# Two transformer blocks on one core: the order of weight roundings, form copies and loads in a Strassen-type feed-forward stage

## The reference

```python
D_FF = (D_MODEL * 11) // 4            # 5632
def conv_ffn(h, up, conv_w, conv_b, down):
    hid = causal_dwconv(h @ up.astype(h.dtype), conv_w, conv_b)   # 3 taps along positions
    gate, val = jnp.split(hid, 2, axis=-1)
    return (jax.nn.gelu(gate) * val) @ down.astype(h.dtype)
...
        h = rms_norm(x, pre_ffn_norm[l])
        y = conv_ffn(h, ffn_up[l], ffn_conv_w[l], ffn_conv_b[l], ffn_down[l])
        x = x + rms_norm(y, post_ffn_norm[l])
```

## Time and profile before

| | |
|---|---|
| runs of the kernel | 2668.67 us median of 3 (2666.76 to 2669.28) |
| profiled execution, own time | 2666.55 us |
| its span, first to last instruction | 2664.6 us |
| mean granted clock of TensorE | 0.995 |
| TensorE busy | 2628.2 us (99%) |
| VectorE, ScalarE, GpSimd busy | 1827.3, 1137.3, 309.5 us |
| first up quad, about | 1361 to 1403 us of the span |
| down quads, about | 2180 to 2582 us |
| last segment, about | 2583 to 2665 us |

### The profile page before, as it was taken

One profiled execution on the slowest core, in us unless ns is written; L12 is line 12 of the kernel. 1 busy time (PEld: TensorE's weight loads), 2 busy tenths in 40 slices (PEclk: granted clock), 3 DMA queues, 4 the chain that ended last, 5 costly groups with the idle time before them and its releaser, 6 DMA issues. The chain is left out here.

```text
span 2664.6 us, 39524 instructions
## 1 busy us (share of the span) xinstructions
PE 2628.2 (99%) x17064; PEld 2291.9 (86%) x17064; DVE 1827.3 (69%) x1836; ACT 1137.3 (43%) x1183; POOL 309.5 (12%) x338
## 2 busy tenths in 40 slices
PE   9999999999999999999999999999999999999998
PEld 8778877878888888788889999999999987777787
DVE  6556467773554666523897787787787796788884
ACT  5335255632522333422554444344444455434445
POOL 1003100350000000011010000000000001212203
PEclk9999999999999999999999999999999999999998
DMA  6225411452232221232377777787777777888843
GB/s 232 87 87 193 131 64 64 158 180 95 85 105 85 95 80 60 75 140 99 152 199 183 199 202 185 205 197 187 208 189 194 210 200 235 241 232 245 214 149 111
DMA packets 119499, 416.70 MB, mean 156 GB/s; under 512 B 8208, under 2 KB 72848, under 8 KB 80544
## 3 DMA queue, kind: packets, MB, share of 16 engines
q1 hardware_dynamic: 94800, 271.76, 28.8%
q0 software_dynamic: 24240, 142.16, 23.8%
q10 hardware_dynamic: 288, 0.27, 0.0%
HBM read 378.51 MB, written 32.51 MB: 154 GB/s over the span
## 5 line engine op out<-in xcount | busy, mean ns | idle before, releaser
L969 PE MATMUL ps<-h_hi,w_hi 128*128 128x512 f32 x1200 | 481.5, 401 | 0.0
L971 PE MATMUL ps<-h_hi,w_lo 128*128 128x512 f32 x1200 | 468.1, 390 | 0.0
L970 PE MATMUL ps<-h_lo,w_hi 128*128 128x512 f32 x1200 | 467.8, 390 | 0.0
L2629 DVE TENSOR_TENSOR w_lo<-raw,w_hi 128x2048 fp32r<-128x2048 f32 x105 | 246.3, 2346 | 198.5 <-ACT w_hi L1844 198.4
L1721 PE MATMUL ps<-h_hi,w_hi 128*128 128x256 f32 x1280 | 363.2, 284 | 4.3 <-DVE w_lo L3523 4.3
L1722 PE MATMUL ps<-h_lo,w_hi 128*128 128x256 f32 x1280 | 362.9, 284 | 0.0
L1723 PE MATMUL ps<-h_hi,w_lo 128*128 128x256 f32 x1280 | 362.9, 284 | 0.0
L1844 ACT ACTIVATE w_hi<-raw 128x2048 fp32r<-128x2048 f32 x105 | 200.6, 1911 | 362.8 <-PE ps L971 310.5
L3523 DVE TENSOR_TENSOR w_lo<-raw,w_hi 128x2048 fp32r<-128x2048 f32 x91 | 208.4, 2291 | 140.6 <-ACT w_hi L2378 140.5
L2378 ACT ACTIVATE w_hi<-raw 128x2048 fp32r<-128x2048 f32 x91 | 174.4, 1916 | 280.2 <-PE ps L1723 199.8
L969 PEld LDWEIGHTS ps<-h_hi,w_hi 128*128 128x128 f32 x1200 | 225.3, 188 | 57.3 <-issue 11.1
(11 more groups left out here) (567 smaller groups left out, 5526.1 us busy)
## 6 DMA issues: line engine op xcount, KB each, us to landing
raw<-weights SPq DMA_DIRECT2D x142, 1024.0 KB, 4.8
raw<-weights POOLq DMA_DIRECT2D x60, 1024.0 KB, 8.5
X<-weights SPq DMA_DIRECT2D x59, 1024.0 KB, 6.7
q_raw<-weights SPq DMA_DIRECT2D x30, 1024.0 KB, 5.7
q_raw<-weights POOLq DMA_DIRECT2D x30, 1024.0 KB, 8.0
f_spill<-f_val POOLq DMA_DIRECT2D x22, 512.0 KB, 5.4
x_spill<-X POOLq DMA_DIRECT2D x8, 1024.0 KB, 8.9
f_even<-f_spill SPq DMA_DIRECT2D x6, 1024.0 KB, 10.7
```

Of the source, the lines that this page charges most:

```text
L969: pe.matmul(o, w_hi[:, s % 2, w], h_hi[:, t, :], start=(t == 0), stop=False)
L970: pe.matmul(o, w_hi[:, s % 2, w], h_lo[:, t, :], start=False, stop=False)
L971: mm = pe.matmul(o, w_lo[:, s % 2, w], h_hi[:, t, :], start=False, stop=(t == 15))
L2629: V.tensor_tensor(w_lo[:, slot, :], raw[:, slot, :], w_hi[:, slot, :].bitcast(F32), ALU.subtract).then_inc(w_ready, 1)
```

## The change

No instruction is added or taken away on ScalarE, VectorE and TensorE; the order changes in three places. The sums form_1 to form_4 of the gated tiles stay on VectorE.

- First up quad. VectorE does the taps of the first value tile ahead of the remainder of S1, and the remainder of `t3` and the taps of the next gate tile ahead of the remainder of A11. ScalarE's copy of `X[:, 8:16]` moves behind the rounding of A12. GpSimd stores the first gated tile before its 2048-element add. TensorE and SyncE count the forms in the new order.
- Down quads. On VectorE each remainder is followed by the take of the product that freed its slot, and then by at most one or two pieces of form work; form_4 goes from ahead of the sum of A11 to behind the remainder of A11 and a take, form_1 from ahead of the remainder of A12 to behind it, and the rest follows. On ScalarE the copies of the next chunk's S1 and S2 move behind the roundings of A12 and A22. In quad 19 the split of S4 comes before the forms. SyncE loads A11 and A22 of the next quad before the next chunk's gated tiles.
- Last segment. ScalarE does square and gain of a tile together and spreads those of the first half between its takes; turns, the first half's sum and the root's spread move one to three tiles forward on TensorE; VectorE's scaling and residual adds follow one tile earlier.

The diff, cut to its core:

```diff
@@ sync
-                    sp.wait_ge(*form_ready.at(2))
+                    sp.wait_ge(*form_ready.at(3))
+                    sp.wait_ge(*form_made.at(4))
...
+                if q + 1 < ALL_QUADS:
+                    sp.wait_ge(w_ready, at(q, J_S3) + 3)
+                    load_a11(q + 1)
+                    sp.wait_ge(w_ready, at(q, J_A22) + 3)
+                    load_a22(q + 1)
                 if q >= QUADS and q % 2 == 0:
                     ... load_f ...
-                (the same two loads of q + 1)
@@ gpsimd
             sum_r(0)
+            store_f(0)
             pool.wait_ge(*form_made.at(3))
             nc.gpsimd.tensor_tensor(X[:, 8:16, N1], X[:, 8:16, N1], X[:, 0:8, N2], ALU.add).then_inc(form_made.sem, 1)
-            store_f(0)
@@ tensor, last segment
-                            for k in {(0, 1, 3): (0, 1), (0, 2, 3): (2, 3), (0, 3, 3): (4, 5), (1, 0, 1): (6, 7)}.get((half, q, j), ()):
+                            for k in {(0, 1, 3): (0, 1), (0, 2, 1): (2,), (0, 2, 2): (3,), (0, 2, 3): (4,), (0, 3, 3): (5,),
+                                      (1, 0, 1): (6,), (1, 0, 2): (7,)}.get((half, q, j), ()):
                                 turn_out(k)
-                            if (half, q, j) == (1, 1, 0):
+                            if (half, q, j) == (1, 0, 3):
                                 pe.wait_ge(*turn_copied.at(4))
                                 sum_half(0)
@@ scalar, quad
                 if q == 0:
                     gelu(0)
-                    form(X_r[:, 0:8, N1], X[:, 8:16, N1], 4)
+                if q == 0:
+                    first_tap0(1, 0, hid)
...
                 hi(at(q, J_A22), a22_raw)
+                act.wait_ge(*r2_summed[q % 2].at(16 * (q // 2 + 1)))
+                hi(at(q, J_S4), raw[:, q % 2, :])
                 if q == QUADS - 1:
                     form_hi_made(0, J_S1, 1)
                     form_hi_block(0, J_A11, 0, 0)
                     form_hi_made(0, J_S2, 2)
                     form_hi_block(0, J_A12, 1, 0)
@@ scalar, down_quad
-                if p == 1 and c + 1 < CHUNKS:
-                    form_hi_made(c + 1, J_S1, 1)
                 take(q, J_S1)
                 act.wait_ge(*a12_landed.at(16 * (q + 1)))
                 hi(at(q, J_A12), a12_at(q))
                 take(q, J_A11)
                 if p == 1 and c + 1 < CHUNKS:
+                    form_hi_made(c + 1, J_S1, 1)
                     form_hi_block(c + 1, J_A11, 0, 0)
                 act.wait_ge(*q_summed.at(16 * (q + 1)))
                 hi(at(q, J_S3), q_raw[:, :])
                 take(q, J_S2)
-                if p == 1 and c + 1 < CHUNKS:
-                    form_hi_made(c + 1, J_S2, 2)
                 act.wait_ge(*a22_landed.at(16 * (q + 1)))
                 hi(at(q, J_A22), a22_raw)
                 take(q, J_A12)
                 if p == 1 and c + 1 < CHUNKS:
+                    form_hi_made(c + 1, J_S2, 2)
                     form_hi_block(c + 1, J_A12, 1, 0)
@@ vector, quad
+                if q == 0:
+                    first_taps(0, 1, hid_b)
                 lo(at(q, J_S1), raw[:, q % 2, :])
...
                     gated(0)
                     ffn_take_first(5, 4, hid)
+                    form_lo(t3_lo[:, :, :], t3[:, :, :], t3_hi[:, :, :], 2)
+                    first_taps(1, 0, hid)
                     lo(at(q, J_A11), q_raw[:, :])
@@ vector, down_quad
                 if p == 0:
                     form_3(c)
-                    form_4(c)
-                    form_lo_made(c, J_S2, 3)
                 dve.wait_ge(*q_landed.at(16 * (q + 1)))
                 V.tensor_tensor(raw[:, q % 2, :], raw[:, q % 2, :], q_raw[:, :], ALU.add).then_inc(summed.sem, 1)
                 lo(at(q, J_A11), q_raw[:, :])
                 ... finish_gate or take(q - 1, J_S4) ...
+                if p == 0:
+                    form_4(c)
+                    form_lo_made(c, J_S2, 3)
+                lo(at(q, J_S2), raw[:, q % 2, :])
+                take(q, J_S1)
+                if p == 0: form_lo_made(c, J_S3, 5)
                 lo(at(q, J_A12), a12_at(q))
+                take(q, J_A11)
+                if nxt: form_1(nxt)
+                if p == 0: form_lo_made(c, J_A22, 6)
                 lo(at(q, J_S3), q_raw[:, :])
+                take(q, J_S2)
+                if p == 0: form_lo_block(c, J_S4, 1, 1)
+                if nxt: form_lo_block(nxt, J_A11, 0, 0)
                 lo(at(q, J_A22), a22_raw)
+                take(q, J_A12)
+                if nxt: form_2(nxt); form_lo_made(nxt, J_S1, 1)
                 lo(at(q, J_S4), raw[:, q % 2, :])
+                take(q, J_S3)
+                if nxt: form_lo_block(nxt, J_A12, 1, 0)
@@ scalar, last segment
+            def square_gain(half, t):
+                end_square(half, t)
+                if (half, t) == (1, KT - 1):
+                    end_root(1)
+                end_gain(half, t)
...
+                if t in (9, 10):
+                    turn_in(t - 7)
+                for n in {8: (0, 1), 9: (2,), 10: (3,), 11: (4, 5), 12: (6,), 13: (7,), 14: (8,), 15: (9,)}.get(t, ()):
+                    square_gain(0, n)
```

More of the change, by code:

```diff
@@ L2425, in quad @@
                 hi(at(q, J_A12), a12_at(q))
+                if q == 0:
+                    form(X_r[:, 0:8, N1], X[:, 8:16, N1], 4)
                 act.wait_ge(*val_conved.at(q + 2))
@@ L2506, in down_quad @@
                 take(q, J_S3)
+                if q == QUADS:
+                    gelu(q + 1)
             def form(dst, src, n):
@@ L2586, in end_gain @@
                 A(y_acc[:, t, cols], y_acc[:, t, cols], ACT.Identity, scale=par("post_ffn", t)).then_inc(sem("y_gained"), 1)
-            for t in range(12):
+            def square_gain(half, t):
[3 more added lines that the diff above has]
+                end_gain(half, t)
+            for t in range(KT):
                 keep(t)
@@ L2591, in _ @@
                     step_hi_end(N_POS - 2 + t // 4)
-                if t == 9:
-                    for n in range(4):
-                        end_square(0, n)
-            turn_in(2)
-            turn_in(3)
-            for t in range(12, KT):
-                keep(t)
-            for t in range(4, 12):
-                end_square(0, t)
+                if t in (9, 10):
+                    turn_in(t - 7)
+                for n in {8: (0, 1), 9: (2,), 10: (3,), 11: (4, 5), 12: (6,), 13: (7,), 14: (8,), 15: (9,)}.get(t, ()):
+                    square_gain(0, n)
+            for t in range(10, 14):
+                square_gain(0, t)
+            turn_in(6)
+            square_gain(0, 14)
+            turn_in(7)
+            square_gain(0, 15)
             A(credit[:, 10:11], eps_c, ACT.Sqrt)
-            for t in range(12, KT):
-                end_square(0, t)
-            turn_in(6)
-            turn_in(7)
             end_root(0)
             for t in range(KT):
-                end_gain(0, t)
-            for t in range(KT):
-                end_square(1, t)
-                if t == KT - 1:
-                    end_root(1)
-                end_gain(1, t)
+                square_gain(1, t)
             for k in range(4):
@@ L3619, in quad @@
                     form_lo_block(0, J_A12, 1, 0)
-                lo(at(q, J_S4), raw[:, q % 2, :])
             def form_1(c):
@@ L3716, in down_quad @@
                     mix(0, 1)
-                take(q, J_S1)
                 lo(at(q, J_A12), a12_at(q))
+                take(q, J_A11)
+                if nxt:
+                    form_1(nxt)
+                if p == 0:
+                    form_lo_made(c, J_A22, 6)
                 if q == QUADS:
                     val_taps(q - 1)
+                if end:
+                    mix(0, 2)
+                lo(at(q, J_S3), q_raw[:, :])
+                take(q, J_S2)
+                if p == 0:
+                    form_lo_block(c, J_S4, 1, 1)
                 if nxt:
                     form_lo_block(nxt, J_A11, 0, 0)
-                take(q, J_A11)
                 if end:
-                    mix(0, 2)
                     mix(0, 3)
-                lo(at(q, J_S3), q_raw[:, :])
-                if q == QUADS:
-                    gate_taps(q - 1)
-                take(q, J_S2)
+                lo(at(q, J_A22), a22_raw)
+                take(q, J_A12)
                 if nxt:
@@ L3736, in down_quad @@
                     mix(0, 5)
-                lo(at(q, J_A22), a22_raw)
+                lo(at(q, J_S4), raw[:, q % 2, :])
+                take(q, J_S3)
                 if nxt:
                     form_lo_block(nxt, J_A12, 1, 0)
-                take(q, J_A12)
                 if end:
                     mix(0, 6)
-                take(q, J_S3)
-                lo(at(q, J_S4), raw[:, q % 2, :])
-                if end:
                     dve.wait_ge(w_used, at(q, J_S3) + 2)
@@ L3836, in _ @@
                 add_down(t)
-                if t == 5:
+                if t == 4:
                     end_inverse(0)
-                if t in (7, 9, 11, 13):
```

(8 more changed lines are left out.)

39 lines of the change are left out of this document (10 added, 29 removed).

## The result

| | before | after |
|---|---|---|
| median of 6 runs each, us | 2668.07 (2665.78 to 2669.28) | 2676.23 (2673.74 to 2678.70) |
| profiled execution: own time, span, us | 2666.55, 2664.6 | 2673.74, 2671.7 |
| mean granted clock of it | 0.995 | 0.997 |

The ratio is 1.0032, 95% interval 1.0019 to 1.0045: the change makes the kernel 8.2 us slower. I forecast slower by 23. The direction held and the time lies at the low end of the range (2675 to 2708), but the size was nearly three times too large. The profiled run is the lowest of the six; the others have spans up to 2676.7 us at clocks down to 0.995. So a difference of a few us between two profiled executions can be the clock alone.

What follows compares the result with a forecast made beforehand. TensorE, busy 99% of the span, was taken as the bound. +19.5 + 6 + 2 + 0 - 4 = +23.5 on the profiled 2666.55 us gives 2690, plus one: 2691 us; range 2675 to 2708.

Steps and rivals of the forecast that it cites:

- Down quads, +19.5: Down quads and the wait before them: roundings behind late form copies on ScalarE, waits 38.7 us in place of 19.2.
- Rival (c): Down quads: VectorE's backlog, not ScalarE's queue, sets the waits, which fall to 0.2 us each; 2637 us, chance 0.08.
- Clock in the down quads, +6: Down quads: clock falls after the new waits cost 9.4 us, less 3.4 before; bounds -3.4 and +16.
- rival (a): Down quads: the clock holds at full level through the 2 to 3 us waits; about 2682 us, chance 0.18.
- GpSimd's multiplies of x, +2: Down quads: VectorE pieces slowed beside these multiplies may now be form sums on the chain; +2 us, bounds 0 and +6.
- First up quad, 0: Opening: 3.4 us won with the clock, but GpSimd's add delays A11's product some 3.5 us; bounds -4 and +3.
- rival (e): Opening: GpSimd's add does not collide with VectorE; 2687 us, inside the forecast, sharing its chance of 0.55.
- Last segment, -4: Last segment: sums wait about 1 instead of 2.7 and 1.4 instead of 2.0 us, plus some clock; bounds -7 and 0.

Runs made afterwards that it cites:

- e3: The changed kernel with form_4 alone made before VectorE's sum of A11 again in even down quads: 2655.49 us, ratio 0.9958.
- e4: The changed kernel with ScalarE's copies of form_1 to form_4 put behind the roundings they stood ahead of, one VectorE form remainder moved along: 2637.82 us.
- e2: The kernel before with only the change's order of quad 19 and the down quads, its loads and GpSimd's x transfers: 2688.49 us, ratio 1.0085.
- e6: The changed kernel with only the odd down quads' form copies put behind the roundings of S3 and S4 on ScalarE: 2665.61 us.
- e1: The kernel before with only the change's edits of the last segment: 2658.23 us, ratio 0.9965.
- e5: The kernel before with only the change's order of the first up quad: 2668.28 us over ten runs, ratio 1.0005.
- e8: The kernel before with one edit in the last segment, each gain of the first half right behind its square on ScalarE: 2662.16 us, ratio 0.9986.
- e7: e4 with the 2048-element add of the first up quad done by VectorE instead of GpSimd: 2631.79 us.

## Why the prediction was right in direction and wrong in size

- **Down quads, +19.5. The mechanism right, the term 3.5 too large.** The waits came place by place within 0.5 us, 37.7 in all against 38.7. But 38.7 counts each wait from where the product was due, and the 19.2 taken off is idle time alone. Counted the same way it is 21.7 before, so the term is +16.0.
- **Rival (c), VectorE's backlog.** False for this change, by e3 and e4; and the point from which I let it decide was the right one: in e4, where ScalarE's copies are done behind the roundings, the waits are nearly gone. That its time of 2637 is that of e4 (2637.82) is in part luck. It had 4 us from the opening, which did not come (0), and 4 from the end, which gave 11.5.
- **Clock in the down quads, +6.** Too high for the profiled execution. There are 18 waits, and three stretches below full level. Taking length times what is missing to 1.00, as in the prediction, the three rows give 3.5 + 1.8 + 1.8 = 7.1 us; the first fall began inside the wait of 4.84 us, where it costs nothing, and by the products themselves 5.6 are lost. Before it was 3.4, so the term is +2.2. It is not wrong for this order in general: the profiled execution is the fastest of the six, and e2 and e6, which have the same waits at S2, lost 9.9 and 9.4, that is +6.5 and +6.0 (the old order lost 3.1 to 5.1 in its four traces, before, e1, e5 and e8). I had counted four falls in five waits at S2: over after, e2 and e6 there are twelve in fifteen. At S4 I had half; in after and e2 there are none in six. So rival (a), which had 0.18, is nearer for this execution alone. The Trainium skill, "TensorE: Matmul & The Clock Gate", section "HAM oscillation — how this bites in real kernels", tells of a kernel in which each wait for operands brings the engine back at half clock, with waits of 3 to 5 us. The 4.84 us wait agrees; the shorter ones at S2 did so in some cases and not in others.
- **GpSimd's multiplies of x, +2.** Nothing of it shows. The last segment starts 18.6 us later; +16.0 and +2.2, a wait of 0.6 ahead of its first product, which I did not have, and 0.3 sooner at the last up product make 18.5.
- **First up quad, 0.** Right, and by the step given: t3's remainder took 6.53 us beside GpSimd's add (4.63) instead of 2.28, and A11's product waited 2.8 (I had 3.5), then 0.3 and 1.5 for the two later waits (I had 1.1 and 1.9). e5 measures no change, e7 takes the collision away and its opening is 4.2 us shorter. The Trainium skill, "SBUF — State Buffer", section "SBUF: two separate sides", says that the one of the two that starts first holds their shared ports for its whole instruction; here GpSimd's add started first (1357.88 against 1358.14), and 6.53 beside 2.28 agrees with it, so rival (e) fell.
- **Last segment, -4. This step failed.** It measured -11.5. It had two errors. The waits fell from 2.0 and 2.7 at the sums to 0.3 and 0.2, where I had 1.4 and 1.0, and the 0.9 at line 1792 is gone, which I had not counted: 5.1 us won in place of 2.3. And the clock: I had only the row of 2626 to 2632, 2.2 us, and counted part of it. Over the whole segment before, the windows give 62 x 0.06 = 3.7 and 13 x 0.26 = 3.4 us, 7.1 together, and 0.1 after (13 x 0.01). 5.1 + 7.0 = 12.1, 0.6 more than measured; the rounding of the clock to 0.01 leaves 0.3 of it open. The second fall begins within 1 us behind the 2.67 us wait at the last sum, and I never looked behind it. e1 shows the gain by itself, and e8 that half of it (5.9 us) comes with the last sum's wait, most of it as clock.

The sum with the measured terms is +16.0 + 2.2 + 0.6 - 0.3 + 0 - 11.5 = +7.0: +7.1 by the profiles, +8.2 by the medians. The largest error is the end's: 7.5 of the 16.4 us by which the profiles' +7.1 falls short of my +23.5. The rest is 3.8 of clock in the down quads, 3.5 of waits and 2 of GpSimd, less 0.4 of small things that I had not counted. The median lies just inside my range, and that is luck: I had added up its low end of 2675 from rival (a) and the bounds of the clock and of GpSimd, not from an end that gives three times as much.

## What to carry to other kernels

When one engine's work is spread evenly, look at the in-order queue of the engine that consumes it. Here a copy of 1 us that waits for a late sum held a rounding that nothing else held, and its place, not its length, cost 31 of 34 us of waits. A piece that needs a late result belongs behind the piece that the critical engine waits for.

And count the clock over the whole stage around a wait, not at the wait alone: at the end of this kernel 5.6 us of waits carried 7 us of lost clock.

## What the runs showed of the hardware

- The same wait in the same place halves TensorE's clock in one case and not in another. Ahead of S2 TensorE waits 2.5 to 4.8 us, five times each in after, e2 and e6; twelve of these fifteen waits were followed by a stretch at 1.2 GHz that began in the wait or within 2 us behind it, three were not (quads 24 and 28 in after, quad 22 in e2). The waits of 1.95 us ahead of S3 brought none of six in after and e2, and all three in e3. So executions of one kernel differ: spans of 2671.7 to 2676.7 us at mean clocks of 0.997 to 0.995. With few waits the times lie close together: e7 has a clock of 1.000 in its profiled execution and its four runs lie within 1.5 us.
- Beside GpSimd's add of 2048 elements (4.63 us) VectorE's two-input remainder took 6.53 us instead of 2.28. That is about the 4.37 us that the add still ran plus the remainder's own 2.28, as if it had stood still until the add ended.
